# A prefetch hint for the branch that closes TensorE's loop over the expert turns

## The reference, cut to what matters

```python
logits = (xt @ w_router).astype(jnp.float32)
top_logit, top_e = lax.top_k(logits, TOP_K)
gate = jax.nn.softmax(top_logit, axis=-1)
...
def expert_block(args):
    xblk, e = args
    g, u = jnp.split(xblk @ w_in[e], 2, axis=-1)     # w_in[e]: 1024 x 7168, float32
    return (jax.nn.silu(g) * u) @ w_out[e]           # w_out[e]: 3584 x 1024, float32
```

## Time and profile before

| | |
|---|---|
| median of 3 runs | 1404.94 us (1402.66 to 1405.67) |
| the profiled execution's own time | 1403.84 us |
| its span, first to last instruction | 1402.1 us |
| mean granted TensorE clock | 0.978 of full |
| TensorE busy | 1339.9 us, 96% of the span |
| the eight expert turns | 469.26 to 1386.96 us, 917.7 us |

### The profile page before, as it was taken

The page is one execution under the profiler, slowest core; times in us unless marked ns, Lnnn a source line. Parts: engine busy times, 40 slices in busy tenths (PEclk is TensorE's granted clock), DMA queues, the critical chain, the costliest instruction groups (busy, mean ns, idle before and its releaser), DMA issues.

```text
span 1402.1 us, 32399 instructions
## 1 busy us (share of the span) xinstructions
PE 1339.9 (96%) x14455; PEld 738.1 (53%) x14455; DVE 395.9 (28%) x666; ACT 273.7 (20%) x491; POOL 70.1 (5%) x97
## 2 busy tenths in 40 slices
PE   8998999999999999899899989989989998999996
PEld 6875799998867434433433533433343352344344
DVE  5869655554776111011001101101100110120212
ACT  5665454443464000000000010000000001000000
POOL 2033200000032100000000000000000000000100
PEclk9999999999999899999999999999999999999999
DMA  9851269855715999899989989999999998999980
GB/s 313 228 165 61 91 210 336 295 181 194 188 54 211 357 386 418 353 389 418 406 331 419 415 324 414 419 346 389 418 401 339 420 415 326 414 419 401 419 333 32
DMA packets 115787, 443.37 MB, mean 316 GB/s; under 512 B 11936, under 2 KB 49088, under 8 KB 101312
## 3 DMA queue, kind: packets, MB, share of 16 engines
q1 hardware_dynamic: 108704, 423.39, 79.3%
q10 hardware_dynamic: 5792, 13.63, 2.6%
q0 software_dynamic: 1152, 4.19, 0.7%
HBM read 425.85 MB, written 15.34 MB: 315 GB/s over the span
## 4 chain that ended last, share of the span: by engine, by line
PE 92%; DVE 3%; issue 3%; ACT 2%; DMA 0%; DVEq 0%; ACTq 0%
PE bank L1581 43%; PE bank L1574 21%; PE bank L1057 8%; PE bank L1059 7%; PE bank L1058 7%; PE bank L1074 2%; PE bank L1330 1%; ACT arena L901 1%; PE bank L1291 1%; PE bank L1518 1%; ACT wh L723 0%; PE bank L1379 0%; DVE wl L1617 0%; PE bank L1285 0%; PE bank L1401 0%
## 5 line engine op out<-in xcount | busy, mean ns | idle before, releaser
L1581 PE MATMUL bank<-ring,arena 128*32 128x448 f32 x2880 | 292.6, 566 | 29.9 <-issue 29.1
L2050 DVE TENSOR_TENSOR arena<-arena,bank 128x448 f32<-128x448 f32 x48 | 26.9, 617 | 783.5 <-PE bank L1581 783.5
L1581 PEld LDWEIGHTS bank<-ring,arena 128*32 128x32 f32 x2880 | 91.7, 115 | 224.4 <-issue 224.2
L1617 DVE TENSOR_TENSOR wl<-ring,wh 128x2048 fp32r<-128x2048 f32 (+1 forms) x59 | 133.2, 2261 | 86.0 <-ACT wh L723 85.7
L723 ACT ACTIVATE wh<-ring 128x2048 fp32r<-128x2048 f32 (+1 forms) x60 | 113.4, 1892 | 100.4 <-PE bank L1059 97.7
L1574 PE MATMUL bank<-ring,arena 128*32 128x256 f32 x2304 | 125.7, 379 | 0.0
L1581 PE MATMUL bank<-whs,arena 128*32 128x448 f32 x1152 | 111.1, 539 | 0.0
L1581 PE MATMUL bank<-wls,arena 128*32 128x448 f32 x1152 | 111.1, 539 | 0.0
L1006 ACT ACTIVATE arena<-bank 128x448 f32<-128x448 f32 x48 | 22.6, 544 | 437.6 <-PE bank L1581 437.6
L1574 PEld LDWEIGHTS bank<-ring,arena 128*32 128x32 f32 x2304 | 71.1, 110 | 55.8 <-issue 4.0
L1057 PE MATMUL bank<-hTh,wh 128*128 128x256 f32 (+1 forms) x352 | 99.7, 283 | 0.0
(11 more groups left out here) (279 smaller groups left out, 1405.8 us busy)
## 6 DMA issues: line engine op xcount, KB each, us to landing
ring<-in_moe_w_in_dram SPq DMA_DIRECT2D x120, 896.0 KB
ring<-in_moe_w_out_dram SPq DMA_DIRECT2D x48, 1024.0 KB
whs<-in_moe_w_in_dram SPq DMA_DIRECT2D x48, 896.0 KB, 8.4
wls<-in_moe_w_in_dram SPq DMA_DIRECT2D x48, 896.0 KB, 9.2
arena<-in_moe_w_in_dram SPq DMA_DIRECT2D x32, 896.0 KB, 9.0
whs<-in_moe_w_out_dram SPq DMA_DIRECT2D x24, 1024.0 KB, 10.3
wls<-in_moe_w_out_dram SPq DMA_DIRECT2D x24, 1024.0 KB, 11.0
ring<-in_dense_w_in_dram SPq DMA_DIRECT2D x22, 1024.0 KB
```

Source lines behind the costliest of these rows:

```text
L1581: ins = pe.matmul(bank[s + GROUPS * (kind == "u")][32 * j:32 * j + 32, 0:BLOCK], xgT[:, c, 32 * s:32 * s + 32], slot[:, BLOCK * j:BLOCK * ...
L1617: dve.tensor_tensor(wl[:, n % SPLITS, 0:size], slot_of(n)[:, 0:size], wh[:, n % SPLITS, 0:size].bitcast(F32), ALU.subtract).then_inc(split, 1)
L2050: ins = dve.tensor_tensor(act[:, s, :], act[:, s, :], bank[GROUPS + s][:, 0:BLOCK], ALU.mult)
```

## The change

```diff
--- before.py
+++ after.py
@@ -1590,7 +1590,7 @@
             gather()
             pe.wait_ge(plan_ready, 1)
             last = pe.value_load(turns_i[0:1, 0:1], min_val=NE - 1, max_val=GROUPS * NE - 1)
-            with pe.Fori(0, last) as i:
+            with nc.Fori(0, last, engines=bass.OrderedEngineSet([pe.engine]), hint_back_edge=True) as i:
                 expert_step(i)
             expert_step(last, last=True)
             put_back()
```

## The result

The changed kernel takes 1363.73 us (median of 4 runs, 1362.89 to 1365.39), the kernel before 1404.05 us (4 runs): the ratio is 0.9714, 95% interval 0.9697 to 0.9731. The forecast was 1361.7 us, with a range from 1357 to 1389 us. The profiled execution took 1362.89 us, with a span of 1361.1 us: 41.0 us less than the span of before.

What follows compares the result with a forecast made beforehand. TensorE was taken as the bound, stalling at six taken branches while the loop's head is fetched. Savings of 27.9 + 15.3 - 0 - 0 = 43.2 us gave 1361.7 us against the median, range 1357 to 1389 us.

Steps and rivals of the forecast that it cites:

- What bounds the kernel: TensorE, busy 96% of 1402.1 us, stalls 29.1 us in six pieces at taken loop branches, fetching the loop's head.
- Term 1, the stall: At the six taken branches the hint cuts each stall to a rest of 0.2 us: 27.9 us saved.
- Term 2, the clock: In the gate-and-up parts behind the six stalls TensorE's clock stays up: 6 x 2.55 = 15.3 us saved.
- Term 3, the fall-through: Seventh branch, wrongly hinted taken: cost 0, bounds 0 and 7.4 us; the following block's fetch was 5 us behind the branch.
- the sign of the wrong hint: In the profile after, a new gap some 5 us behind the start of the last turn.
- What is late next: Expert weight transfers lose almost all their lead of over 20 us but are just in time: cost 0, up to 5 us.
- The hint does nothing: Rival: the hint is dropped before the branch or acts at once, the six stalls stay, 1405 us; chance 0.13.
- Too late in part: Rival: the prefetch leaves a rest of 1 to 3 us at each back edge, 1374 or 1389 us; chance 0.13.
- The wrong hint costs a stall: Rival: at the loop's end the wrong hint costs a full stall with its clock, 7.4 us, 1369 us; chance 0.13.
- The weights become the bound: Rival: TensorE waits for a DMA in the last two turns, 1362 to 1368 us; chance 0.10.
- Slower: Rival: the hint displaces the second block's fetch, adding a second stall per turn, 44 us more, 1449 us; chance 0.05.
- The hint's own cost: One added instruction in TensorE's queue at the head of seven turns, taken to cost 0.

Runs made afterwards that it cites:

- e1: The changed kernel with the loop's first instruction at slot 0 of a 256-instruction fetch block: 1386.26 us.
- e3: The changed kernel with the loop's first instruction at slot 200 of a 256-instruction fetch block: 1398.12 us.
- e7: The changed kernel with the loop written by hand and the plain hint moved from the body's head to 96 matmuls and weight loads before the branch: 1405.72 us.
- e2: The changed kernel with the loop's first instruction at slot 100 of a 256-instruction fetch block: 1360.89 us.
- e6: The changed kernel again, with the plain hint, five runs: 1365.15 us, ratio to the kernel before 0.9721.
- e9: The changed kernel with TensorE made to wait at each turn's head for ScalarE's eviction, which ScalarE precedes with five extra copies: 1409.42 us.
- e4: The changed kernel with the loop written by hand and the hint's outcome taken from a register, so the last turn is hinted rightly: 1362.47 us.
- e5: The changed kernel with both the hint's outcome from a register and the loop's head at slot 100, five runs: 1359.94 us, ratio to before 0.9687.
- e8: The changed kernel with TensorE's loop over turns 0 to 6 written out as seven copies, with no branch: 1360.94 us.

## Why the prediction was right, point by point

**What bounds the kernel** held: nearly all of the change is in the six places that it named. The span fell by 41.0 us, and the rows give 27.2 + 15.1 + 0.5 - 1.9 = 40.9 us of it. Against the forecast of 43.2 us the stall gave 0.7 us less, the clock 0.2 us less and the last turn 1.9 us less; the 0.5 us is luck (below).

**Term 1, the stall** (27.9 us): 29.13 - 1.94 = 27.2 us. The rest was to be 0.2 us and is 0.32 on average: the restart comes 2.9 to 3.05 us after the fetch, and not the 2.8 us taken over from the stall. The reason held too: the target is fetched where the next block in line was fetched, 2.7 us ahead of the end of work, and one fetch less is needed for each taken branch. e1 to e3 show that this distance sets the rest, and e7 that a hint 96 instructions ahead of the branch comes too late. That the forecast total of this wait, under 1.5 us, became 3.3 us is due to the gap of the last turn (1.37 us) and to the longer rests. The favourable rest was luck with the layout; by the slot alone the change is worth between 7 us (e3) and 44 us (e2).

**Term 2, the clock** (15.3 us): 449.3 us in six gate-and-up parts (74.70 to 75.14 each) against 6 x 72.37 = 434.2 us, so 15.1 us. Rests up to 0.8 us left the clock alone (e6) and those from 2.1 us did not in e1, but in e3 rests of 2.70 and 3.13 us, each with a second gap behind it, left it at 1.00; what decides between 0.8 and 3.1 us no run here shows. e9 shows the fall with no fetch involved. The first turn, which I left out, was 0.5 us shorter (74.31 against 74.81). That is not the change's doing: the same part takes 75.02 us in e6, the same kernel.

**Term 3, the fall-through** (0 us, bounds 0 and 7.4): 1.9 us, the term that was mis-sized. Its step "a fetch begun at the branch would have most of these 5 us" failed. The missing block is fetched 3.5 us behind the branch, near the end of the block that holds it (e2 moved that end, and the gap went with it). Its place, some 5 us into the last turn, was named in advance as the sign of the wrong hint. It costs less than a full stall, 1.4 us of gap and not 4.9, because this fetch starts 1.0 us before TensorE runs dry, and in the stalls of the kernel before it started 1.6 to 2.3 us after; the restart then took 2.4 us here and 2.8 us there. Why it starts earlier is not shown; that TensorE's queued matmuls last longer there (0.094 us a record against 0.054) is an argument only. e4 shows that the whole of it is the wrong hint.

**What is late next**: the forecast that the transfers lose most of their lead and are just in time was right for the profiled execution, with 7.1 us left; 13.0 us in e6 says that it was somewhat pessimistic.

**The rivals.** "The hint does nothing" is what e7 measures, but only for a hint that comes too late. "Too late in part" is e1 and e3: it was one layout away. "The wrong hint costs a stall" happened at a quarter of its price. "The weights become the bound" did not happen even with 12 slots. "Slower" did not happen; its second gap a few us into the turn exists (e3), but only where the loop's head stands near the end of a block, and there the stall at the branch was shortened all the same.

**The hint's own cost** (taken as 0): e5, with the hint and two register operations in each turn, and e8, with neither, have no gap in any turn, and their turns take 871.6 and 871.5 us.

## What to carry to other kernels

A gap with releaser "issue" at each return to a loop's head, and none where the loop falls through, suggests the fetch of the head; a packet of the instruction queue inside the gap confirms it (here it starts 2.8 to 2.9 us before TensorE works again). Count it twice, once as a stall and once for the slow clock behind it (here 4.9 + 2.5 us each time). Hint the branch at the head of the body; 96 instructions ahead of the branch was too late here. Then look at two places: the gaps that remain at the head (move the loop within its fetch block: here slot 100 left no gap at any head, slots 0 and 200 left 2.1 to 3.7 us) and a new gap shortly behind the loop's exit (take the hint's outcome from a register, so that the last turn is not hinted wrongly).

## What the runs showed that I had not expected

The place of the loop within a fetch block moved the time of a hinted loop from 1398 us (slot 200) over 1386 (slot 0) to 1361 us (slot 100), and by nothing without the hint (1404.5 us). And the seventh, wrongly hinted branch costs only 1.9 us. Each taken branch gives back (27.2 + 15.1) / 6 = 7 us, so by this estimate the hint pays in the changed kernel's layout from the first taken branch on.
